# First two weight units in halves, feature rows one by one, and five products ahead on TensorE

## The chip, the cores and the metric

The kernel runs on one core of a Trainium2 chip. Its time is the device time of that core in microseconds (us), from the first to the last instruction. One execution is profiled; the others are only timed. In the names of the profile PE is TensorE's matmul, PEld its weight load, DVE is VectorE, ACT is ScalarE, POOL is GpSimd, SPq is SyncE's queue of DMA issues.

## What is computed

A trunk of two layers over 512 positions and 1024 features, in float32. Each layer adds half a feed-forward block, a mixer and another half of a feed-forward block to x, and an RMS norm ends the trunk. This case plays in the first feed-forward block:

```
def rmsnorm(x, w, eps=NORM_EPS):
    xf = x.astype(F32)
    y = xf * lax.rsqrt(jnp.mean(xf * xf, axis=-1, keepdims=True) + eps)
    return (y * w.astype(F32)).astype(x.dtype)

def swiglu(x, w_gate, w_up, w_down):
    return (jax.nn.silu(x @ w_gate) * (x @ w_up)) @ w_down
...
    for l in range(DEPTH):
        i = l // 2
        x = x + 0.5 * swiglu(rmsnorm(x, ffn_norm[l, 0]), ffn_w_gate[l, 0], ffn_w_up[l, 0], ffn_w_down[l, 0])
```

## The kernel before

x lies in `X` with features down the partitions: 8 rows of 128 features by 512 positions (256 KB each). The weights come in units. A unit of `w_gate` or `w_up` is 128 output features by 1024 inputs, 512 KB, and makes one bank of 128 by 512 results. Units alternate: 0 gate, 1 up, 2 gate, 3 up, and so on. SyncE loads units into the four slots of `RAW`, and a load waits until DVE has made the low part of the unit that held the slot (`lo_ready`).

Each product in full precision is done as three products on numbers split in two. ACT rounds the raw weights to the high part (`split_hi`, line 1340, counted by `hi_ready`), DVE subtracts it from the raw weights for the low part (`split_lo`, line 1989, counted by `lo_ready`). Both go to `WS`, which has two slots, so ACT may split unit 2 only when PE has done unit 0 (`unit_done`). x is split the same way into `H`, after a multiplication by the norm's weight: ACT line 1431 (`hhi_ready`), DVE line 2073 (`h_ready`). Of the pair of semaphores of such a name one counts even rows and one odd rows. For each of the 8 rows of a unit PE then does high by high, high by low and low by high (lines 614 to 616), 24 products of 512 columns in a unit.

The division by the root of the mean square is done on the results. So PE can start before it is known. ACT squares the rows of `X` (line 1350) into `US[:, 0]` and `US[:, 1]` in turn, DVE adds seven of them to `ACC` (line 2087), and `norm_sum` on PE (lines 655 and 656) sums `ACC` and the eighth over the features with two products in plain float32. ACT takes the root, DVE the reciprocal (line 2020), and then each bank is scaled, which sets it free. There are two gate and two up banks. POOL clears `ACC` at the very start (line 1860, `acc_clear`).

The order at the start is written by hand, engine by engine:
- SyncE: parameters (`PRM`), unit 0, x in four loads of two rows with unit 1 behind the first, unit 2, the constants (`CST`), unit 3.
- ACT and DVE: unit 0, rows 0 and 1, unit 1, rows 2 to 7, with squares between, then unit 2.
- PE (`first_units`): rows 0 and 1 of unit 0, rows 0 and 1 of unit 1, rows 2 to 7 of unit 0, rows 2 to 7 of unit 1; two rows of unit 2, `norm_sum`, the other six rows, unit 3. After this all phases go on by loops that count units.

## Time and profile before

| | us |
|---|---|
| median of 3 timed runs | 2102.22 |
| their range | 2101.36 to 2102.86 |
| the profiled execution (its span is its time) | 2102.0 |
| PE busy | 2062.4, 98% of the span |
| DVE busy | 1131.0, 54% |
| ACT busy | 780.5, 37% |

The profiled execution lies 0.2 us under the median. Starts are counted from the start of the span. In a timeline, a row gives start, length, engine, line, operation, what it writes and reads, and in brackets how long the engine had been idle and what ended that. Neighbours of one kind are merged into one row with a count. The lengths of pipelined products overlap, so what a product costs is read from the starts.

### The profile page before, as it was taken

To read this page: it belongs to the slowest core of one execution; us is meant where nothing else is said; L and a number is where in the kernel's file an instruction comes from. 1 tells how busy PE (TensorE), PEld (TensorE's weight loads), DVE (VectorE), ACT (ScalarE), POOL (GpSimd) and SP (SyncE) were. 2 spreads that over 40 slices of the span, in tenths; PEclk is the share of its full clock that TensorE was granted. 3 is DMA by queue.
4 is the path that set the end of the run, shared out by engine and by line. 5 is a ranking of instruction groups with operands and counts; after the bars stand their busy time and mean duration, and the time that the engine had idled before them with its cause. 6 is when DMAs were issued, how large, how long until landed. Compare 5 with 4: busy or idle time off the path is not lost.

```text
span 2102.0 us, 33182 instructions
## 1 busy us (share of the span) xinstructions
PE 2062.4 (98%) x13322; PEld 1699.5 (81%) x13322; DVE 1131.0 (54%) x1463; ACT 780.5 (37%) x1182; POOL 160.7 (8%) x118
## 2 busy tenths in 40 slices
PE   8999999999799999999999999999999999999998
PEld 6888888777768888888888888877888888888886
DVE  6444444678767444444444443469777675444322
ACT  5233223483434223322323232246665453233221
POOL 0000011002302000011000001101111120000010
PEclk9999999999999999999999999999999999999999
DMA  5222322320022222322222232221111122222321
GB/s 183 100 93 97 113 96 81 106 78 14 11 74 91 100 99 91 115 97 89 91 94 95 100 109 98 86 80 62 51 51 42 58 86 99 100 90 100 111 97 52
DMA packets 48265, 182.65 MB, mean 87 GB/s; under 512 B 6320, under 2 KB 6576, under 8 KB 48048
## 3 DMA queue, kind: packets, MB, share of 16 engines
q1 hardware_dynamic: 48176, 181.39, 25.1%
q8 instruction: 65, 1.06, 0.2%
q14 instruction: 24, 0.20, 0.0%
HBM read 179.27 MB, written 2.10 MB: 86 GB/s over the span
## 4 chain that ended last, share of the span: by engine, by line
PE 69%; DVE 2%; ACT 1%; issue 0%; POOL 0%; DVEq 0%; ACTq 0%; POOLq 0%
PE banks L614 21%; PE banks L615 21%; PE banks L616 21%; PE banks L1225 1%; PE banks L1194 0%; PE banks L1176 0%; PE banks L1264 0%; PE banks L1047 0%; PE banks L1266 0%; PE banks L1245 0%; PE banks L1242 0%; PE banks L1150 0%; PE banks L1130 0%; PE banks L1006 0%; DVE WS L1989 0%
## 5 line engine op out<-in xcount | busy, mean ns | idle before, releaser
L614 PE MATMUL banks<-H,WS 128*128 128x512 f32 x1840 | 727.6, 395 | 8.4 <-DVE H L2073 8.0
L615 PE MATMUL banks<-H,WS 128*128 128x512 f32 x1840 | 717.0, 390 | 0.0
L616 PE MATMUL banks<-H,WS 128*128 128x512 f32 x1840 | 716.9, 390 | 0.0
L1340 ACT ACTIVATE WS<-RAW 128x1024 fp32r<-128x1024 f32 (+1 forms) x306 | 345.0, 1128 | 909.4 <-PE banks L616 905.5
L1989 DVE TENSOR_TENSOR WS<-RAW,WS 128x1024 fp32r<-128x1024 f32 (+1 forms) x306 | 400.9, 1310 | 193.6 <-ACT WS L1340 193.2
L614 PEld LDWEIGHTS banks<-H,WS 128*128 128x128 f32 x1840 | 345.7, 188 | 85.1 <-DVE WS L1989 9.2
L616 PEld LDWEIGHTS banks<-H,WS 128*128 128x128 f32 x1840 | 345.7, 188 | 72.5
L615 PEld LDWEIGHTS banks<-H,WS 128*128 128x128 f32 x1840 | 345.9, 188 | 70.2 <-issue 1.2
L614 PE MATMUL banks<-A,WS 128*128 128x512 f32 x704 | 273.9, 389 | 0.0
L616 PE MATMUL banks<-A,WS 128*128 128x512 f32 x704 | 273.9, 389 | 0.0
L615 PE MATMUL banks<-A,WS 128*128 128x512 f32 x704 | 273.9, 389 | 0.0
L2029 DVE TENSOR_TENSOR US<-banks,RSTD 128x512 f32<-128x512 f32 x88 | 60.8, 691 | 252.2 <-PE banks L616 252.2
L1855 POOL TENSOR_TENSOR ACC<-ACC,US 128x512 f32<-128x512 f32 x47 | 87.5, 1862 | 1402.5 <-issue 763.0
L2029 DVE TENSOR_TENSOR GS<-banks,RSTD 128x512 f32<-128x512 f32 x88 | 60.8, 691 | 179.9 <-PE banks L616 179.8
L614 PEld LDWEIGHTS banks<-A,WS 128*128 128x128 f32 x704 | 132.1, 188 | 27.5
L616 PEld LDWEIGHTS banks<-A,WS 128*128 128x128 f32 x704 | 132.1, 188 | 27.5
L615 PEld LDWEIGHTS banks<-A,WS 128*128 128x128 f32 x704 | 132.1, 188 | 27.3
L2001 DVE SCALAR_TENSOR_TENSOR X<-banks,X 128x512 f32 (+1 forms) x48 | 33.0, 688 | 159.2 <-PE banks L616 159.2
L1380 ACT ACTIVATE A<-US 128x512 f32 (+1 forms) x88 | 55.8, 634 | 46.9 <-DVE US L2036 46.6
L2036 DVE TENSOR_TENSOR US<-GS,US 128x512 f32<-128x512 f32 x88 | 60.9, 692 | 9.1
L2041 DVE TENSOR_TENSOR A<-US,A 128x512 f32 (+1 forms) x88 | 60.2, 685 | 2.8 <-ACT A L1380 2.8
L1375 ACT ACTIVATE GS<-GS 128x512 f32<-128x512 f32 x88 | 54.1, 615 | 10.7 <-DVE GS L2029 10.7
(406 smaller groups left out, 1657.6 us busy)
## 6 DMA issues: line engine op xcount, KB each, us to landing
RAW<-in_w_gate SPq DMA_DIRECT2D x88, 512.0 KB, 3.2
RAW<-in_w_up SPq DMA_DIRECT2D x88, 512.0 KB, 3.2
RAW<-in_w_down SPq DMA_DIRECT2D x64, 704.0 KB, 4.0
RAW<-in_c_in SPq DMA_DIRECT2D x32, 512.0 KB, 3.2
RAW<-in_ab_in SPq DMA_DIRECT2D x22, 512.0 KB, 3.2
RAW<-in_ab_out SPq DMA_DIRECT2D x8, 512.0 KB, 5.0
RAW<-in_c_out SPq DMA_DIRECT2D x8, 512.0 KB, 3.2
X<-in_x SPq DMA_DIRECT2D x4, 512.0 KB, 7.5
```

The source lines that it names most:

```text
L614: pe.matmul(bank[:, :], high[:, cols], upper, start=first and j == 0, stop=False)
L615: pe.matmul(bank[:, :], high[:, cols], lower, start=False, stop=False)
L616: mm = pe.matmul(bank[:, :], low[:, cols], upper, start=False, stop=last and j == len(rows) - 1)
L1340: act.activation(WS[:, 0, c % SPLIT, 0:cols] if dst is None else dst, RAW[:, c % RING, 0:cols], ACT.Copy).then_inc(hi_ready, 1)
L1375: act.activation(GS[:, j, :], GS[:, j, :], ACT.Silu).then_inc(silu_ready[j], 1)
L1380: act.activation(A[:, 0, 2 * i + j, :], US[:, j, :], ACT.Copy).then_inc(ahi_ready[j], 1)
L1855: pool.tensor_tensor(ACC[:, :], ACC[:, :], US[:, j, :], ALU.add).then_inc(acc_ready[j], 1)
L1989: vec.tensor_tensor(WS[:, 1, c % SPLIT, 0:cols], RAW[:, c % RING, 0:cols], WS[:, 0, c % SPLIT, 0:cols].bitcast(F32), ALU.subtract).then_in ...
L2001: vec.scalar_tensor_tensor(X[:, 2 * i + j, :], bank[:, :], factor, X[:, 2 * i + j, :], ALU.mult, ALU.add).then_inc(x_ready[j], 1)
L2029: vec.tensor_tensor((GS, US)[k][:, j, :], (GATE, UP)[k][j][:, :], RSTD[:, :], ALU.mult).then_inc((gs_ready, us_ready)[k][j], 1)
L2036: vec.tensor_tensor(US[:, j, :], GS[:, j, :], US[:, j, :], ALU.mult).then_inc(prod_ready[j], 1)
L2041: vec.tensor_tensor(A[:, 1, 2 * i + j, :], US[:, j, :], A[:, 0, 2 * i + j, :].bitcast(F32), ALU.subtract).then_inc(act_ready[j], 1)
```

## The change

The first two units are loaded and split in two halves of 512 columns, that is of four input rows each. x is loaded row by row. Loads, splits and rows follow each other in one order on SyncE, ACT and DVE. PE takes rows 0 to 2 alternating between gate and up, then rows 3 to 7 of the gate unit and of the up unit, and waits for each row and half by itself. Ahead of all that PE does five products of 256 columns on the cleared `ACC`, into bank 7, which nobody reads; DVE waits for them before it adds to `ACC`. The squares all stand behind the last row now, with unit 2's split after the first two of them. `norm_sum` stands behind five rows of unit 2 and no longer behind two.

The diff:

```diff
--- before.py
+++ after.py
@@ -233,7 +233,12 @@
             return ctx.enter_context(nc.semaphore(name))
 
         landed = sem("constants_landed")
-        x_landed = [sem(f"x_landed{i}") for i in range(KB // 2)]
+        row_landed = [sem(f"row_landed{r}") for r in range(KB)]
+        params_landed = sem("params_landed")
+        half_landed = [sem(f"half_landed{c}") for c in range(2)]
+        half_hi, half_lo = [sem(f"half_hi{c}") for c in range(2)], [sem(f"half_lo{c}") for c in range(2)]
+        warmed = sem("warmed")
+        HALF_COLS = (slice(0, KB // 2 * P), slice(KB // 2 * P, KB * P))
         w_landed = [sem(f"weights_landed{s}") for s in range(RING)]
         hi_ready = sem("weights_hi_ready")
         lo_ready = sem("weights_lo_ready")
@@ -543,12 +548,25 @@
                     sp.wait_ge(lo_ready, u - RING + 1)
                 sp.dma_start(RAW[:, slot, 0:cols], src).then_inc(w_landed[slot], 16)
 
-            sp.dma_start(PRM[:, :], params).then_inc(x_landed[0], 16)
-            load(0, 0, *units[0])
-            for i in range(KB // 2):
-                sp.dma_start(X[:, 2 * i:2 * i + 2, :], x[:, 2 * i:2 * i + 2, :]).then_inc(x_landed[i], 16)
-                if i == 0:
-                    load(1, 1, *units[1])
+            def half_load(c, k):
+
+                sp.dma_start(RAW[:, c, HALF_COLS[k]], units[c][0][:, HALF_COLS[k]]).then_inc((half_landed, w_landed)[k][c], 16)
+
+            def row_load(r):
+
+                sp.dma_start(X[:, r, :], x[:, r, :]).then_inc(row_landed[r], 16)
+
+            half_load(0, 0)
+            sp.dma_start(PRM[:, :], params).then_inc(params_landed, 16)
+            row_load(0)
+            half_load(1, 0)
+            row_load(1)
+            row_load(2)
+            half_load(0, 1)
+            row_load(3)
+            half_load(1, 1)
+            for r in range(4, KB):
+                row_load(r)
             load(2, 2, *units[2])
             sp.dma_start(CST[:, :], const).then_inc(landed, 16)
             for phase in plan:
@@ -630,13 +648,34 @@
 
             def first_units(phase):
 
+                def row(k, r):
+
+                    pe.wait_ge(h_ready[r % 2], r // 2 + 1)
+                    if r < KB // 2:
+                        pe.wait_ge(half_lo[k], 1)
+                    else:
+                        pe.wait_ge(lo_ready, k + 1)
+                    bank, cols = (GATE[0], UP[0])[k], slice(r * P, (r + 1) * P)
+                    pe.matmul(bank[:, :], WS[:, 0, k, cols], H[:, 0, r, :], start=r == 0, stop=False)
+                    pe.matmul(bank[:, :], WS[:, 0, k, cols], H[:, 1, r, :], start=False, stop=False)
+                    mm = pe.matmul(bank[:, :], WS[:, 1, k, cols], H[:, 0, r, :], start=False, stop=r == KB - 1)
+                    if r == KB - 1:
+                        mm.then_inc(unit_done, 1)
+
+                pe.wait_ge(acc_clear, 1)
+                for _ in range(5):
+                    mm = pe.matmul(BANK[7][:, 0:SEQ // 2], ACC[:, 0:P], ACC[:, 0:SEQ // 2], start=True, stop=True)
+                mm.then_inc(warmed, 1)
                 c = base[phase]
-                for rows in ((0, 1), range(2, KB)):
-                    for k, bank in enumerate((GATE[0], UP[0])):
-                        unit(bank, c + k, 0, H_PARTS, rows, rows[0] == 0, rows[0] > 0, norm=0, at_col=rows[0], done=rows[0] > 0)
-                unit(GATE[1], c + 2, 0, H_PARTS, range(2), True, False, done=False)
+                for r in range(3):
+                    for k in range(2):
+                        row(k, r)
+                for k in range(2):
+                    for r in range(3, KB):
+                        row(k, r)
+                unit(GATE[1], c + 2, 0, H_PARTS, range(5), True, False, done=False)
                 norm_sum(0)
-                unit(GATE[1], c + 2, 0, H_PARTS, range(2, KB), False, True, at_col=2)
+                unit(GATE[1], c + 2, 0, H_PARTS, range(5, KB), False, True, at_col=5)
                 unit(UP[1], c + 3, 0, H_PARTS, range(KB), True, True)
 
             def norm_sum(n):
@@ -1423,23 +1462,34 @@
             step = Steps(act, act_step)
             act.wait_ge(acc_clear, 1)
             act.activation(SMALL[:, 0, :], ACC[:, 0:4], ACT.Square)
-            split_hi(0, 0)
-            for i in range(KB // 2):
-                act.wait_ge(x_landed[i], 32 if i == 0 else 16)
+            def half_split_hi(c, k):
+
+                act.wait_ge((half_landed, w_landed)[k][c], 16)
+                act.activation(WS[:, 0, c, HALF_COLS[k]], RAW[:, c, HALF_COLS[k]], ACT.Copy).then_inc(hi_ready if k else half_hi[c], 1)
+
+            def row_hi(r):
+
+                w = norm_cols[0] + r
+                act.wait_ge(row_landed[r], 16)
+                act.activation(H[:, 0, r, :], X[:, r, :], ACT.Copy, scale=PRM[:, w:w + 1]).then_inc(hhi_ready[r % 2], 1)
+
+            half_split_hi(0, 0)
+            act.wait_ge(params_landed, 16)
+            row_hi(0)
+            half_split_hi(1, 0)
+            row_hi(1)
+            row_hi(2)
+            half_split_hi(0, 1)
+            row_hi(3)
+            half_split_hi(1, 1)
+            for r in range(4, KB):
+                row_hi(r)
+            square(0, 0, 0)
+            square(0, 0, 1)
+            split_hi(2, 0)
+            for i in range(1, KB // 2):
                 for j in range(2):
-                    w = norm_cols[0] + 2 * i + j
-                    act.activation(H[:, 0, 2 * i + j, :], X[:, 2 * i + j, :], ACT.Copy,
-                                   scale=PRM[:, w:w + 1]).then_inc(hhi_ready[j], 1)
-                if i == 0:
-                    split_hi(1, 0)
-                if i == 1:
-                    for j in range(2):
-                        square(0, 0, j)
-            for i, j in ((1, 0), (1, 1), (2, 0)):
-                square(0, i, j)
-            split_hi(2, 0)
-            for i, j in ((2, 1), (3, 0), (3, 1)):
-                square(0, i, j)
+                    square(0, i, j)
             split_hi(3, 0)
             act.activation(SMALL[:, 1, :], PRM[:, 0:4], ACT.Sqrt, scale=0.0)
             for phase in plan:
@@ -2065,17 +2115,31 @@
                 vec.tensor_tensor(by_head(INV[z]["IU"]), two_banks(4 * z), minus_by_head(2 << l), ALU.mult).then_inc(iu_ready[z], 1)
 
             step = Steps(vec, vec_step)
-            split_lo(0, 0)
-            for i in range(KB // 2):
-                for j in range(2):
-                    w = norm_cols[0] + 2 * i + j
-                    vec.wait_ge(hhi_ready[j], i + 1)
-                    vec.scalar_tensor_tensor(H[:, 1, 2 * i + j, :], X[:, 2 * i + j, :], PRM[:, w:w + 1],
-                                             H[:, 0, 2 * i + j, :].bitcast(F32), ALU.mult, ALU.subtract).then_inc(h_ready[j], 1)
-                    vec.sem_inc(hw_ready[j], 1)
-                    vec.sem_inc(x_ready[j], 1)
-                if i == 0:
-                    split_lo(1, 0)
+            def half_split_lo(c, k):
+
+                vec.wait_ge(hi_ready if k else half_hi[c], c + 1 if k else 1)
+                vec.tensor_tensor(WS[:, 1, c, HALF_COLS[k]], RAW[:, c, HALF_COLS[k]],
+                                  WS[:, 0, c, HALF_COLS[k]].bitcast(F32), ALU.subtract).then_inc(lo_ready if k else half_lo[c], 1)
+
+            def row_lo(r):
+
+                w = norm_cols[0] + r
+                vec.wait_ge(hhi_ready[r % 2], r // 2 + 1)
+                vec.scalar_tensor_tensor(H[:, 1, r, :], X[:, r, :], PRM[:, w:w + 1],
+                                         H[:, 0, r, :].bitcast(F32), ALU.mult, ALU.subtract).then_inc(h_ready[r % 2], 1)
+                vec.sem_inc(hw_ready[r % 2], 1)
+                vec.sem_inc(x_ready[r % 2], 1)
+
+            half_split_lo(0, 0)
+            row_lo(0)
+            half_split_lo(1, 0)
+            row_lo(1)
+            row_lo(2)
+            half_split_lo(0, 1)
+            row_lo(3)
+            half_split_lo(1, 1)
+            for r in range(4, KB):
+                row_lo(r)
 
             def square_added(i, j):
 
@@ -2087,10 +2151,11 @@
                 vec.tensor_tensor(ACC[:, :], ACC[:, :], US[:, j, :], ALU.add).then_inc(acc_ready[j], 1)
 
             vec.wait_ge(acc_clear, 1)
-            for i, j in ((0, 0), (0, 1), (1, 0), (1, 1), (2, 0)):
-                square_added(i, j)
+            vec.wait_ge(warmed, 1)
+            square_added(0, 0)
+            square_added(0, 1)
             split_lo(2, 0)
-            for i, j in ((2, 1), (3, 0)):
+            for i, j in ((1, 0), (1, 1), (2, 0), (2, 1), (3, 0)):
                 square_added(i, j)
             vec.wait_ge(landed, 16)
             for phase in plan:
```

DVE's program, from its beginning. `WS<-RAW,WS` is a low part of weights (1024 columns are a unit, 512 a half), `H<-X,PRM,H` the low part of a feature row, `ACC<-ACC,US` a sum of squares. Before:

```order
L1989 TENSOR_TENSOR WS<-RAW,WS 128x1024
L2073 SCALAR_TENSOR_TENSOR H<-X,PRM,H 128x512 x2
L1989 TENSOR_TENSOR WS<-RAW,WS 128x1024
L2073 SCALAR_TENSOR_TENSOR H<-X,PRM,H 128x512 x6
L2087 TENSOR_TENSOR ACC<-ACC,US 128x512 x5
L1989 TENSOR_TENSOR WS<-RAW,WS 128x1024
L2087 TENSOR_TENSOR ACC<-ACC,US 128x512 x2
L1989 TENSOR_TENSOR WS<-RAW,WS 128x1024
```

And now:

```order
L2121 TENSOR_TENSOR WS<-RAW,WS 128x512
L2128 SCALAR_TENSOR_TENSOR H<-X,PRM,H 128x512
L2121 TENSOR_TENSOR WS<-RAW,WS 128x512
L2128 SCALAR_TENSOR_TENSOR H<-X,PRM,H 128x512 x2
L2121 TENSOR_TENSOR WS<-RAW,WS 128x512
L2128 SCALAR_TENSOR_TENSOR H<-X,PRM,H 128x512
L2121 TENSOR_TENSOR WS<-RAW,WS 128x512
L2128 SCALAR_TENSOR_TENSOR H<-X,PRM,H 128x512 x4
L2151 TENSOR_TENSOR ACC<-ACC,US 128x512 x2
L2039 TENSOR_TENSOR WS<-RAW,WS 128x1024
L2151 TENSOR_TENSOR ACC<-ACC,US 128x512 x5
```

Row 0 stands behind half a unit, not a whole one; unit 2's split stands behind two sums, not five.

SyncE's DMA issues at the start of the program, before (128x1024 is 512 KB):

```order
L546 DMA PRM<-in_params 128x243
L544 DMA RAW<-in_w_gate 128x1024
L549 DMA X<-in_x 128x1024
L544 DMA RAW<-in_w_up 128x1024
L549 DMA X<-in_x 128x1024 x3
L544 DMA RAW<-in_w_gate 128x1024
L553 DMA CST<-in_const 128x2112
```

And now:

```order
L553 DMA RAW<-in_w_gate 128x512
L560 DMA PRM<-in_params 128x243
L557 DMA X<-in_x 128x512
L553 DMA RAW<-in_w_up 128x512
L557 DMA X<-in_x 128x512 x2
L553 DMA RAW<-in_w_gate 128x512
L557 DMA X<-in_x 128x512
L553 DMA RAW<-in_w_up 128x512
L557 DMA X<-in_x 128x512 x4
L549 DMA RAW<-in_w_gate 128x1024
```

The bytes ahead of unit 2 are the same; they go out as 13 issues in place of 7.

## Rows read from the trace of the kernel before

**Rows 1.** The page's busy times, the first engine

```profile
PE 2062.4 (98%) x13322; PEld 1699.5 (81%) x13322; DVE 1131.0 (54%) x1463; ACT 780.5 (37%) x1182; POOL 160.7 (8%) x118
```

**Rows 2.** Timeline of PE, 0 to 25 us: start, length, what

```profile
7.95 0.77 PE L614 MATMUL banks<-H,WS 128*128 128x512 f32 x1 [7.95 <-DVE H L2073]
...
10.85 0.59 PE L614 MATMUL banks<-H,WS 128*128 128x512 f32 x1
11.28 0.40 PE L615 MATMUL banks<-H,WS 128*128 128x512 f32 x1
11.52 0.39 PE L616 MATMUL banks<-H,WS 128*128 128x512 f32 x1
...
20.40 0.39 PE L616 MATMUL banks<-H,WS 128*128 128x512 f32 x1
20.67 0.50 PE L614 MATMUL banks<-H,WS 128*128 128x512 f32 x1
...
22.16 1.05 PE L655 MATMUL banks<-ACC,CST 128*128 128x512 f32 x2
...
24.14 0.40 PE L615 MATMUL banks<-H,WS 128*128 128x512 f32 x1
```

**Rows 3.** Busy times by stretch: length, then PE, PEld, DVE, ACT, POOL, PEclk, DMA

```profile
7.95:10.65 2.70, 2.70 (x6) 1.80 (x6) 1.60 (x2) 1.93 (x3) 0.00 (x0) 1.00 0.99 352
...
515.00:526.00 11.00, 9.19 (x290) 8.92 (x284) 7.07 (x12) 1.73 (x3) 10.84 (x10) 0.84 0.01 4
```

**Rows 4.** Timeline of DVE, 5 to 30 us

```profile
7.06 1.41 DVE L2073 SCALAR_TENSOR_TENSOR H<-X,PRM,H 128x512 fp32r<-128x512 f32 x2
...
12.80 2.74 DVE L2073 SCALAR_TENSOR_TENSOR H<-X,PRM,H 128x512 fp32r<-128x512 f32 x4 [0.68 <-ACT H L1431]
15.46 3.87 DVE L2087 TENSOR_TENSOR ACC<-ACC,US 128x512 f32<-128x512 f32 x5
...
20.53 1.48 DVE L2087 TENSOR_TENSOR ACC<-ACC,US 128x512 f32<-128x512 f32 x2
...
24.86 3.35 DVE L2020 RECIPROCAL RSTD<-RSTD 128x512 f32<-128x512 f32 x1 [0.71 <-ACT RSTD L1369]
```

**Rows 5.** Timeline of ACT, 4 to 15 us

```profile
4.83 1.06 ACT L1340 ACTIVATE WS<-RAW 128x1024 fp32r<-128x1024 f32 x1 [2.59 <-DMA RAW<-in_w_gate]
6.10 1.33 ACT L1431 ACTIVATE H<-X,PRM 128x512 fp32r<-128x512 f32 x2 [0.21 <-DMA X<-in_x]
8.48 1.06 ACT L1340 ACTIVATE WS<-RAW 128x1024 fp32r<-128x1024 f32 x1 [1.05 <-DMA RAW<-in_w_up]
9.78 1.33 ACT L1431 ACTIVATE H<-X,PRM 128x512 fp32r<-128x512 f32 x2 [0.24 <-DMA X<-in_x]
...
12.06 2.55 ACT L1431 ACTIVATE H<-X,PRM 128x512 fp32r<-128x512 f32 x4
```

**Rows 6.** Timeline of SyncE's DMA issues: the first and the seventh

```profile
0.75 0.40 SPq L546 DMA_DIRECT2D PRM<-in_params  x1
...
3.75 0.45 SPq L549 DMA_DIRECT2D X<-in_x  x1
```

**Rows 7.** Those two in the DMA view: count, KB, us from issue to landing

```profile
PRM<-in_params SPq DMA_DIRECT2D x1, 121.5 KB, 2.2
...
X<-in_x SPq DMA_DIRECT2D x1, 512.0 KB, 8.7
```

**Rows 8.** The page's groups: 512-column operations of the split's kind

```profile
L1380 ACT ACTIVATE A<-US 128x512 f32 (+1 forms) x88 | 55.8, 634 | 46.9 <-DVE US L2036 46.6
...
L2041 DVE TENSOR_TENSOR A<-US,A 128x512 f32 (+1 forms) x88 | 60.2, 685 | 2.8 <-ACT A L1380 2.8
```

**Rows 9.** Timeline of POOL: the clearing of the accumulator

```profile
0.74 0.52 POOL L1860 MEMSET ACC<- 128x512 f32 x1 [0.29 <-POOLq L2687]
```

**Rows 10.** DMA view, 2.0 to 12.4 us, then 381.8 to 384.3 us

```profile
DMA packets 1076, 3.65 MB, mean 351 GB/s; under 512 B 115, under 2 KB 210, under 8 KB 1073
...
DMA packets 309, 0.63 MB, mean 253 GB/s; under 512 B 32, under 2 KB 32, under 8 KB 309
```

## The prediction

> **What bounds the kernel now.** I read the page's busy times first: TensorE (PE) is busy for 98% of the span [rows 1]. A microsecond saved elsewhere is worth nothing unless PE stood waiting for it, and one saved ahead of PE's first product reaches the end in full if no later wait swallows it. So the second view is PE's timeline at the start. The first product of the kernel starts at 7.95 us, and until then PE has done nothing. After that the reader should look at the step from one product to the next. At 10.85 it is 0.43 us (to 11.28), which is 512 columns at 1.2 GHz; from 11.52 to 20.40 there are 39 steps, so 0.228 us each, the 2.4 GHz level [rows 2]. The opening 6 products take the 2.70 us from 7.95 to 10.65. The granted-clock column reads 1.00 there too, so here the steps show the clock and the column does not [rows 3]. Third, the engines that feed PE. VectorE (DVE) has the low part of the last feature row at 12.80 + 2.74 = 15.54 us [rows 4]. ScalarE (ACT) takes each piece the moment it lands, at 4.83, 6.10, 8.48 and 9.78 us, each time after a wait on a DMA [rows 5]. So the opening is bound by arriving data.
>
> From 7.95 to unit 2's first product at 20.67 lie 48 products, 12.72 us; at 0.228 us they need 10.94. Thus 1.78 us go to the slow clock and to waits, and 0.12 more behind 20.67, where six steps of 0.228 take 1.49 us to 22.16 [rows 2].
>
> **Arrival.** Bytes queued decide arrivals. Cumulated in queue order in KB: parameters 122, unit 0 634, first x pair 1146, unit 1 1658, second pair 2170, third 2682, fourth 3194. They land at 0.75 + 2.2 = 2.95 us (parameters), 4.83, 6.10, 8.48, 9.78 (ACT's starts), and the last at 3.75 + 8.7 = 12.45 [rows 5 to 7]. The change queues the same bytes in halves; seven issues went out in the 3.0 us to 3.75, so an issue costs 0.5 us, 256 KB per 0.5 us, faster than the data moves (351 GB/s) [rows 6, 10]. I therefore read the new landings off the same curve, by straight lines between its points: gate half 3.44, row 0 at 4.83, up half 5.46, row 1 at 6.10, row 2 at 7.29, second gate half 8.48, row 3 at 9.13, second up half 9.78, rows 4 to 7 at 10.45, 11.1, 11.8 and 12.45. For the 256 KB of the gate half this is an estimate from the rows at 2.95 and 4.83.
>
> **Cost of the pieces.** A 512-column split is not in the opening, but the same operation on a 512-column tile is: 0.634 us on ACT and 0.685 on DVE [rows 8]. A feature row is 0.71 us on ACT, at a pace of 2.55/4 = 0.64; on DVE 0.746, pace 2.74/4 = 0.685 [rows 4, 5]; one engine's instructions overlap by some 0.07 us. ACT has the gate half at 4.07 and row 0 at 4.83 + 0.71 = 5.54; DVE the gate half's low part at 4.8 and row 0 at 6.32. Before, row 0's low part was ready at 7.06 + 0.75 = 7.81 and PE started 0.14 later. **So the first product comes at 6.46 instead of 7.95: 1.49 us.** What goes is the wait for the whole unit's two splits, of which the second blocked DVE until 7.1 us.
>
> **The race behind it.** Carried on the same way, DVE ends the up half at 6.93, row 1 at 7.61, row 2 at 8.78, row 3 at 10.62, row 4 at 11.94, rows 5 to 7 at 12.6, 13.3 and 13.98. A row of one unit is 3 products, 0.683 us. From 6.46 PE does rows 0 to 2 of both units in 4.10 us, to 10.56; waits 0.16 for row 3 and 0.64 for row 4 (ready 11.94 + 0.1); then finds rows 5, 6 and 7 as it arrives. Row 7 starts at 14.1, and 6 row steps are left: unit 2 could start at 14.1 + 6 x 0.683 = 18.2. **Sum of this stretch: 1.49 (start) + 1.78 (old losses) - 0.80 (new waits) = 2.47 us.** New waits are late data, not weights.
>
> **The five products** read the cleared accumulator, ready at 0.74 + 0.53 = 1.27 us [rows 9]. Their cost is bounded by the kernel's own products in this number form: two of 512 columns fill 22.16 to 24.14 less one 0.228 step, 0.88 us each at 2.4 GHz [rows 2]. At half the columns 0.44, at half the clock 0.88; five take 4.4 us, to about 5.8, under the 6.46 at which data is there. I take that value. The upper end is 1.76 us each, if 256 columns took as long as 512, which ends at 10.1. No lower end matters, because they hide under the data wait. What they buy is the clock: before, the fast level came at about 11.3 us, after seven products had kept PE busy nearly without a break since 7.95; the five keep it busy from 1.4 to 5.8 us, for longer, and end before the data is there, so I take the fast level from 6.46 on. DVE's new wait for them stands behind row 7 (13.98 us), long after: nothing.
>
> **Unit 2, the squares and the norm.** ACT may split unit 2 when unit 0 is done, 14.1 + 0.68 + 0.15 = 14.95, to 16.0; DVE to 17.3; PE wants it at 18.2. Covered by 0.9 us, and the old 0.12 goes. Then five sums remain on DVE, 3.87 us by the row of five [rows 4], to 21.1. PE, with five rows of unit 2 ahead of the sum over features, comes there at 18.2 + 5 x 0.683 = 21.6: covered by 0.5 us (before, 22.01 against 22.16). The extra three rows ahead of it are only moved, but they delay the sum: it starts 0.55 us earlier, not 2.5. The reciprocal behind it ended at 24.86 + 3.35 = 28.2 [rows 4], now at about 27.65, and its first bank is drained by 28.4. PE needs that bank after 3 + 8 more row steps, 21.6 + 1.75 + 7.5 = 30.9. Slack 2.5 us. The loads of units 4 and later start by DVE's splits and arrive long before use. Nothing after this point is touched.
>
> **Sum:** 2.47 + 0.12 = 2.59 us off the profiled execution's 2102.0: 2099.4. That execution is 0.2 us under the median of the timed runs and 0.66 above the fastest, so I take its sum as it is.
>
> **A rule against the trace.** The last 3194 KB land without a fixed cost between pieces: 512 KB takes 1.27 us from 4.83 to 6.10 [rows 5]. The Trainium skill, DMA: Bandwidth & Descriptors, Rules for kernel authors, asks for at least 1 MiB per DMA for bandwidth, and its section on the anatomy of one DMA fits 2.0 us plus the bytes at 436 GB/s; its rule speaks against halves. If the fixed parts did not overlap, 13 transfers would cost an estimated 30 us or more by that page and the kernel would end near 2120; this trace disagrees for queued transfers, so the rule only stands beside rival C.
>
> **The rivals.**
> - A, the forecast: 2099.4.
> - B, **the clock is not up when the data comes.** Between the five products (5.8) and the first real one lies an idle 0.7 us, and the early rows have waits. In 515 to 526 us of this trace the granted clock is 0.84 amid waits and small products [rows 3], so it can fall. If it stays at 1.2 GHz until 11.3 as before, 4.8 us run at half speed, 2.4 us lost, of which 0.8 falls into the data waits: +1.6, 2101.0. Against it: before, the clock rose through six products with a short wait among them.
> - C, **the halves move slower; this one ends above before.** Rows of 2 KB instead of 4 KB on the memory side. Until 12.4 us 3.65 MB moved at 351 GB/s; in a stretch with 2 KB loads in it, 253 GB/s [rows 10]. At that rate the same bytes take 14.4 us from 2.0, row 7 lands at 16.4 and not 12.45, and all behind it moves by 4.0: 2103.4. It decides from about 280 GB/s on (row 7 at 15.0 is break-even); beyond 0.2% slower it would have to be near 210. Against it: that stretch has just started its queue and carries still smaller pieces.
> - D, **more than forecast.** If rows come so smoothly that PE never waits, 0.8 us more; if the run resembles the fastest of before (0.66 lower), 2098.0. For it: the slow stretch of before may last longer in executions other than the profiled one. The Trainium skill, TensorE: Matmul & The Clock Gate, says that the number of slow matmuls at a kernel's start varies from run to run (Part 1, on the clock gate); it gives 6, 11 and 14 for one kernel. By that page alone an estimate is up to 8 x 0.2 = 1.6 us of more gain. One trace can't show it.
> - E, **the five products hold PE.** At 1.76 us each the first real product waits until 10.1, then runs fast: unit 2 at 21.0, 2102.3.
> - F, **the gain is given back later:** unit 3's split or the bank of unit 4 late after all. 2102.0.
>
> **How the numbers follow.** A 0.70, B 0.08, C 0.04, D 0.12, E 0.03, F 0.03. Predicted 2099.4. The range 2097.8 to 2101.6 holds A, B and D, and leaves C, E and F out, 0.1 plus what may lie outside by unknown cost. A measurement of this kernel tells 0.2% from no change, 4.2 us: below 2098.0 or above 2106.4. Faster by that: most of D, 0.10. Slower by that: half of C, 0.02. Within: 0.88.
>
> **What would show it.** In the profile after: first real product near 6.5; step 0.228 from there or from shortly after; small waits before rows 3 and 4, none by weights; row 7's low part near 14.0; unit 2's first product near 18.2; no wait at the feature sum. A row 7 landing past 13 us speaks for C, steps of 0.43 after 6.5 for B, a first product after 7 with idle DVE for E. The prediction is wrong if the 16 DMA engines don't serve the halves in the order queued, since every time above hangs on that curve.

## The result: 6.5 us slower

| | before | after |
|---|---|---|
| median of 7 timed runs, us | 2102.03 | 2108.52 |
| their range | 2101.33 to 2102.86 | 2107.25 to 2109.36 |
| span of the profiled execution | 2102.0 | 2106.6 |

The ratio is 1.003 with a 95% interval of 1.0021 to 1.0039. 2.6 us of gain were forecast. In every run here the time lies about 1.8 us above the span (2108.42 and 2106.6 for the profiled execution of after). The profiled execution of before is therefore not a typical one: by its span of 2102.0 its time must be near 2103.8, above all seven timed runs, and it holds a stretch at the lower clock at 520 us (granted clock 0.56 from 519.4 to 523.3). A second trace of the same kernel (b_again, span 2099.6, time 2101.41) lacks that stretch, and I compare with it where it says so; its time lies 0.4 to 1.1 us under the medians of before, so it is one of the faster ones. Two executions of b_tail32 (2307 and 4862 us) and one of before beside them (2566 us) were disturbed and are left out below.

**Where the time went.** I laid the starts of ScalarE's some 300 weight splits of the two traces side by side; how late a kernel is by this measure I call its lag. Against b_again, after is about 2.8 us late from 40 us on and stays so until 490 us; in the first mixer, 495 to 600 us, it loses 4.2 more; after that nothing changes up to the end: 7.0 = 2106.6 - 2099.6. So there are two places, the opening and the mixer, and the second has not one edited line in it.

**The first place.** The timeline of PE in after: start, length, line, what it writes and reads, and in brackets how long it was idle and what ended that. The five products are the first row (ten records).

```profile
1.32 3.98 PE L667 MATMUL banks<-ACC 128*128 128x256 f32 x10 [1.32 <-POOL ACC L1910]
6.86 0.50 PE L659 MATMUL banks<-H,WS 128*128 128x512 f32 x1 [1.57 <-DVE H L2128]
7.20 0.40 PE L660 MATMUL banks<-H,WS 128*128 128x512 f32 x1
...
8.86 0.47 PE L659 MATMUL banks<-H,WS 128*128 128x512 f32 x1 [1.02 <-DVE WS L2121]
...
13.54 0.50 PE L659 MATMUL banks<-H,WS 128*128 128x512 f32 x1 [0.30 <-DVE H L2128]
...
19.87 0.39 PE L632 MATMUL banks<-H,WS 128*128 128x512 f32 x1
...
23.27 1.02 PE L694 MATMUL banks<-ACC,CST 128*128 128x512 f32 x2
...
34.46 0.50 PE L632 MATMUL banks<-H,WS 128*128 128x512 f32 x1 [1.79 <-DVE WS L2039]
...
35.29 0.63 PE L632 MATMUL banks<-H,WS 128*128 128x512 f32 x1
...
38.67 0.39 PE L634 MATMUL banks<-H,WS 128*128 128x512 f32 x1
```

PE begins at 6.86 in place of 7.95 [rows 2], runs at 2.4 GHz at once (7.20 to the next at 7.44), and reaches unit 2 at 19.87, 0.8 ahead of before. The sum over features (L694) comes at 23.27, 1.1 later than the 22.16 of before: three more rows stand ahead of it, 2.05 us of work, which use up the lead of 0.8 and more. (Without them it could have come 0.4 sooner at most, since DVE's last sum, which it needs, ends at 22.80; see a_norm2.) At unit 4 PE waits 1.79 us for DVE's low part. Then, from 35.29 to 38.67, eight steps take 3.38 us, 0.42 each: the 1.2 GHz level. Eight at 0.228 are 1.82, so this costs 1.56 more. The same unit began at 33.52 in before, without a wait; 34.46 - 33.52 + 1.56 = 2.5 us. PE's timeline and DVE's in before, unit 4's first product and its split:

```profile
33.52 0.50 PE L614 MATMUL banks<-H,WS 128*128 128x512 f32 x1
```

```profile
32.24 1.22 DVE L1989 TENSOR_TENSOR WS<-RAW,WS 128x1024 fp32r<-128x1024 f32 x1
```

DVE's timeline in after says why unit 4 is late.

```profile
12.73 2.77 DVE L2128 SCALAR_TENSOR_TENSOR H<-X,PRM,H 128x512 fp32r<-128x512 f32 x4
15.42 1.48 DVE L2151 TENSOR_TENSOR ACC<-ACC,US 128x512 f32<-128x512 f32 x2
17.79 1.22 DVE L2039 TENSOR_TENSOR WS<-RAW,WS 128x1024 fp32r<-128x1024 f32 x1 [0.89 <-ACT WS L1379]
18.93 3.87 DVE L2151 TENSOR_TENSOR ACC<-ACC,US 128x512 f32<-128x512 f32 x5
...
25.81 3.35 DVE L2070 RECIPROCAL RSTD<-RSTD 128x512 f32<-128x512 f32 x1 [0.86 <-ACT RSTD L1408]
...
32.59 0.68 DVE L2079 TENSOR_TENSOR GS<-banks,RSTD 128x512 f32<-128x512 f32 x1
33.19 1.22 DVE L2039 TENSOR_TENSOR WS<-RAW,WS 128x1024 fp32r<-128x1024 f32 x1
```

The last feature row's low part ends at 15.50, before at 15.54 [rows 4]: all that begins earlier ahead of it ends at the same time. Behind it DVE even falls back. Only two of its sums now stand ahead of unit 2's low part, and that waits for ACT's split (16.70, itself released by PE's end of unit 0), so DVE idles 0.89 us before 17.79; in before five sums stood there, until 19.33 [rows 4], and the low part followed at 19.39. Its last sum ends at 22.80 against 22.01, and root and reciprocal follow (25.81 against 24.86 [rows 4]), then the scalings of units 0 and 1, and behind them stands unit 4's split, 33.19 to 34.41.

**The second place** is seen in waits that the profile lays to "issue", which means that nothing it shows was waited for. PE's timeline from 495 to 605 us in after has three:

```profile
535.38 0.33 PE L774 MATMUL banks<-IU,XT 64*64 64x64 f32 x2 [1.02 <-issue]
567.13 0.45 PE L774 MATMUL banks<-IU,XT 64*64 64x64 f32 x12 [1.15 <-issue]
580.60 0.62 PE L1014 MATMUL banks<-VT,KBT 64*64 64x64 f32 x14 [0.96 <-issue]
```

b_again has one, at the same product as the third:

```profile
573.61 0.62 PE L975 MATMUL banks<-VT,KBT 64*64 64x64 f32 x14 [0.95 <-issue]
```

Here PE runs hundreds of products of 64 columns. Behind the first stall of after the clock is low: 32 such products take 1.13 us at 537.02 and 0.69 at 542.13 (timeline of after).

```profile
537.02 1.13 PE L774 MATMUL banks<-IU,XT 64*64 64x64 f32 x32
...
542.13 0.69 PE L774 MATMUL banks<-IU,XT 64*64 64x64 f32 x32
```

The stalls are 3.1 us against 0.95, so 2.2 of the 4.2; the rest, 2.0, is this stretch (granted clock 0.66 from 536 to 541 us) and what waits for it, which I did not divide further. The third stall is no part of the loss: it stands at the same product, the 8852nd from the end of PE's program, and lasts 0.95 to 0.96 us in every one of the fourteen traces of this case.

**The loads.** DMA by stretch, 4 to 7 us, in before and then in after (length; busy us of PE, PEld, DVE, ACT, POOL; clock; share of the DMA engines; GB/s):

```profile
4.00:7.00 3.00, 0.00 (x0) 0.00 (x0) 1.08 (x1) 1.96 (x3) 0.00 (x0) 1.00 0.99 344
```

```profile
4.00:7.00 3.00, 1.43 (x6) 0.88 (x5) 1.44 (x2) 0.89 (x2) 0.00 (x0) 1.00 0.79 216
```

The halves and rows start well and then fall behind. The single rows of x have a share in this: in the same stretch the other kernels that load them so have 243 to 260 GB/s (a_split4, a_trim_nowarm, a_nowarm), a_pairs, which has half weights but x in pairs, has 325, and b_again 391. ACT's timeline in after shows when it could take what had landed: gate half 3.54, row 0 at 5.30, up half only at 7.35.

```profile
3.54 0.63 ACT L1468 ACTIVATE WS<-RAW 128x512 fp32r<-128x512 f32 x1 [1.30 <-DMA RAW<-in_w_gate]
5.30 0.72 ACT L1474 ACTIVATE H<-X,PRM 128x512 fp32r<-128x512 f32 x1 [1.13 <-DMA X<-in_x]
7.35 0.63 ACT L1468 ACTIVATE WS<-RAW 128x512 fp32r<-128x512 f32 x1 [1.33 <-DMA RAW<-in_w_up]
```

### The profile page after: what moved, and what is told of

Same layout as the page of the kernel before. It is cut to its first block, busy times and chain, and to the rows that moved or that the text cites. A ratio compares the mean times of both kernels' runs of the same rounds, so it can differ in the third digit from the quotient of the medians.

```text
span 2106.6 us, 33225 instructions
## 1 busy us (share of the span) xinstructions
PE 2067.7 (98%) x13332; PEld 1703.3 (81%) x13332; DVE 1132.4 (54%) x1465; ACT 781.4 (37%) x1184; POOL 160.7 (8%) x118
## 4 chain that ended last, share of the span: by engine, by line
PE 69%; DVE 2%; ACT 1%; issue 0%; POOL 0%; DVEq 0%; ACTq 0%; POOLq 0%
PE banks L632 21%; PE banks L633 21%; PE banks L634 21%; PE banks L1264 1%; PE banks L1233 0%; PE banks L1215 0%; PE banks L1303 0%; PE banks L1086 0%; PE banks L1305 0%; PE banks L1284 0%; PE banks L1281 0%; PE banks L1189 0%; PE banks L1169 0%; PE banks L1045 0%; DVE HF L2740 0%
```

## The experiments

The two theories: S, **the split of unit 4** stands at the end of a chain that the change made end later, while PE comes there earlier (theory 1 in the expectations below); P, **the place in the program** (theory 3): the change puts 32 instructions into PE's program ahead of the mixer (20 for the five products, 12 for rows that wait for two semaphores; of 64 bytes each, by the length of the compiled program, 1,073,216 bytes before and 2048 more after), and at which products PE has to wait for its instructions depends on that. Their rivals were the five products themselves, the smaller loads (theory 2), and chance from run to run. The runs came in three groups with runs of before on the same chip beside them, whose medians were 2102.52 (26 runs), 2101.79 (15) and 2102.51 (35).

### a_split4: after, unit 4's split ahead of the scalings

```diff
+                        elif first:
+                            split_hi(4, 0)
...
+                        if first and not base[phase]:
+                            split_lo(4, 0)
                         scaled(phase, i, j, 0)
```

At its old place, behind the scalings, unit 4's split is left out on both engines; that part of the edit is not shown.

> The changed kernel with one thing moved: on ScalarE and VectorE the split of weight unit 4 stands right behind the root and the reciprocal, ahead of the first bank's scaling, and no longer behind it. Theory 1 (the feature sum comes 1.1 us later than before, since five rows of unit 2 stand ahead of it, and with it unit 4's split; PE then waits 1.79 us at 32.5 us and its clock falls to the lower level for 8 products, 1.6 us): the wait and the slow stretch are gone, the time is 3.4 us under the changed kernel, about 2105.1. Theory 2 (the halved loads are slow and that is all): no difference, 2108.5. Theory 3 (the five products or the longer program cost time in later phases): no difference here either.

Measured: 2107.76 (2104.63 to 2110.44, 10 runs), ratio 1.0023 (1.0014 to 1.0033); profiled span 2104.3. The wait at unit 4 is gone from the trace, as DVE's timeline shows: the split is the first thing behind the reciprocal.

```profile
26.57 3.36 DVE L2072 RECIPROCAL RSTD<-RSTD 128x512 f32<-128x512 f32 x1 [0.84 <-ACT RSTD L1408]
29.96 1.22 DVE L2041 TENSOR_TENSOR WS<-RAW,WS 128x1024 fp32r<-128x1024 f32 x1
```

At 390 us this execution is level with b_again (-0.1 us), though it fell to the lower clock once in its first waits (steps of 0.43 from 9.35 to 11.91). In the mixer it then loses 4.8. So the trace bears S out for the first place; S says nothing of the second. The timed runs alone don't show it: the median moved by 0.8 where 3.4 were expected, and the interval overlaps that of after. Three of the ten runs lie at 2104.6 to 2104.9 with a mean granted clock of 0.998, the others at 2106.1 and more with 0.995 to 0.997, so the low clock comes and goes between runs. The timed proof of S is the last experiment.

### a_norm2: after, the sum over features behind two rows again

```diff
-                unit(GATE[1], c + 2, 0, H_PARTS, range(5), True, False, done=False)
+                unit(GATE[1], c + 2, 0, H_PARTS, range(2), True, False, done=False)
                 norm_sum(0)
-                unit(GATE[1], c + 2, 0, H_PARTS, range(5, KB), False, True, at_col=5)
+                unit(GATE[1], c + 2, 0, H_PARTS, range(2, KB), False, True, at_col=2)
```

> The changed kernel with the feature sum behind two rows of unit 2, as before, instead of five. Theory 1: PE gets there at 21.2 us and waits for the sums of squares, which end at 22.8, so the sum starts at 22.9 instead of 23.27; unit 4's split comes 0.4 us earlier and the total waits of PE are about the same: 2108.1, between 2106.5 and 2108.5. If instead the five rows alone were the cause, the feature sum would start near 21.3 and the time come out at 2104 or less.

Measured: 2109.39 (2106.80 to 2112.79, 7 runs), ratio 1.0035 (1.0024 to 1.0047). PE's timeline:

```profile
23.13 1.10 PE L694 MATMUL banks<-ACC,CST 128*128 128x512 f32 x2 [1.54 <-DVE ACC L2151]
```

The wait at unit 4 is gone and stands at the sum instead, 1.54 us. The sum starts at 23.13 where it started at 23.27: DVE sets it, not PE. Taking the three rows away brings the sum only 0.14 us; what then holds it is DVE's last sum, which ends at 23.03 in this trace behind a gap of 1.96 ahead of unit 2's low part. PE's lead can be taken back at either place, but it is taken back. The time is above the 2106.5 to 2108.5 that I expected: the opening of this execution loses only 1.3 us against b_again, with no low clock behind the wait, but the mixer 6.3, with a fourth stall.

### a_nowarm: after without the five products

```diff
-                pe.wait_ge(acc_clear, 1)
-                for _ in range(5):
-                    mm = pe.matmul(BANK[7][:, 0:SEQ // 2], ACC[:, 0:P], ACC[:, 0:SEQ // 2], start=True, stop=True)
-                mm.then_inc(warmed, 1)
```

> The changed kernel without the five products ahead and without VectorE's wait for them. Theory 1: the first products run at the lower clock for some 3.4 us from 6.9 us on, the waits for rows swallow a part; PE reaches the feature sum up to 1 us later (up to 24.3 us), and everything behind follows: 2108.5 to 2109.5. Theory 3 (these products cost time later by the longer program): up to 2 us faster, 2106.5.

Measured: 2107.76 (2106.19 to 2108.75, 8 runs), ratio 1.0025 (1.0014 to 1.0036). The first 6.5 us of products go at 0.43 each, unit 2 comes at 21.21, and unit 4's wait of 1.79 us is there to the digit, with the lower clock behind it. In the mixer, where its displacement is 12 instructions in place of 32, it loses 1.8 and not 4.2. In the traces the five products win about 1.3 us at unit 2, and 2.4 more are lost in the mixer with the 20 instructions that they are; the two medians (0.8 apart) have intervals that overlap.

### b_warm: before with the five products and DVE's wait for them, nothing else

```diff
+                pe.wait_ge(acc_clear, 1)
+                for _ in range(5):
+                    mm = pe.matmul(BANK[7][:, 0:SEQ // 2], ACC[:, 0:P], ACC[:, 0:SEQ // 2], start=True, stop=True)
+                mm.then_inc(warmed, 1)
...
             vec.wait_ge(acc_clear, 1)
+            vec.wait_ge(warmed, 1)
```

> The kernel before with nothing but the five products ahead (and VectorE's wait for them). PE starts at full clock at 7.95 us and could be 1.2 us ahead at the end of the first two units. Theory 1 (the chain of splits, sums, root, reciprocal and unit 4's split on VectorE bounds the opening, PE's lead is taken back at unit 2's split, ready at 20.6 us): nothing gained, 2102.0, within 0.5; a fall of the clock in the new wait could make it 1 to 2 us slower. If PE alone bounded the opening: 2100.8. Theory 3 (later phases pay for the longer program): 2103.5 to 2104.

Measured: 2104.65 (2103.54 to 2107.70, 10 runs), ratio 1.0011 (1.0001 to 1.0021). At 390 us it is 0.3 ahead of b_again, so the clock gain at the start was real, and most of it was taken back: a wait of 0.53 for the up unit's weights, then unit 2 at 20.06 right behind the end of its low part (20.01), 0.6 ahead, and unit 4 at 32.91, right behind the end of its own (32.86), 0.6 ahead. In the mixer it loses 3.5. **This is an edit of the first microseconds whose cost lies in the mixer, with a stall of 1.34 at 562 us.**

### b_pad32 and b_pad128: before with increments of an unused semaphore at PE's head

```diff
+                for _ in range(32):
+                    pe.sem_inc(warmed, 1)
                 c = base[phase]
```

> The kernel before with 32 semaphore increments that nobody waits for at the head of PE's program, where PE is idle until 8 us; its PE program is then exactly as long as the changed kernel's (32 instructions of 64 bytes more). Theory 3, sharpened (PE's instructions are fetched in pieces of 16 KB, and in the mixer stretch at 500 to 600 us, with many short products, PE stands still where a fetch comes late; a longer head moves these places): the opening is as before, the stretch 500 to 600 us has the changed kernel's stalls of issue (3.1 us against 1.6 in the profile before), 1.5 to 3 us slower, 2104 to 2105.5. Theory 1 alone (only the opening matters): 2102.5, as before.

Measured: 2107.62 (2106.51 to 2108.53, 9 runs), ratio 1.0027 (1.0017 to 1.0037). The loads, splits, products and their order are those of before, and PE was idle where the increments stand. The loss, 5.8 us, is nearly that of the whole change and more than the 1.5 to 3 I expected. PE's timeline from 495 to 605 us:

```profile
533.48 0.32 PE L738 MATMUL banks<-IU,XT 64*64 64x64 f32 x2 [1.02 <-issue]
546.70 0.33 PE L867 MATMUL banks<-FACTORS,AL 64*64 64x64 f32 x5 [1.13 <-issue]
565.88 0.45 PE L738 MATMUL banks<-IU,XT 64*64 64x64 f32 x12 [1.15 <-issue]
579.35 0.62 PE L978 MATMUL banks<-VT,KBT 64*64 64x64 f32 x14 [0.96 <-issue]
```

The first, third and fourth are the three of after: the same products (2 left of one group, 12 of another), the same lengths. The second has none beside it in after, but one in a_norm2. 0.9 us are lost in the opening, 4.8 in the mixer.

b_pad128 has `range(128)` there.

> The same with 128 increments, half a piece of 16 KB. Theory 3: other stalls again, a time that differs from the kernel before and from the one with 32, between 2102 and 2106. Theory 1 alone: 2102.5.

Measured: 2117.50 (2117.25 to 2119.23, 4 runs), ratio 1.0075 (1.0059 to 1.0092). This one is half spoilt as a test: the 128 increments last until 20.50 us, 0.16 each, and so hold PE's first product back by 12 us. Behind that the mixer loses 3.1. Two stalls stand at other products again (1.56 at 545.47, 1.10 at 575.89); the third (589.88) is the one that all traces have.

### b_again: before once more

> The kernel before once more, for a second profile: the first has a stretch at the lower clock in the mixer (519.9 to 523.3 us) and lies 1.3 us above the median of the timed runs of before. Expected span 2100.7, without that stretch; the stalls of issue in 500 to 600 us at the same lines as in the first profile if they belong to the program.

Measured: 2101.41, span 2099.6, no stretch at the lower clock at 520 us. Of the first trace's three stalls (0.21 at 531.19, 0.43 at 560.78, 0.95 at 576.20) only the last is there; so a place decides where a stall can fall, not that it does.

### a_pairs: after with x in four loads of two rows

```diff
-                sp.dma_start(X[:, r, :], x[:, r, :]).then_inc(row_landed[r], 16)
+                sp.dma_start(X[:, r:r + 2, :], x[:, r:r + 2, :]).then_inc(row_landed[r], 16)
```

> The changed kernel with x loaded in four pairs of rows, as before, and only the weights in halves; the rest of the order is the same. Theory 2 (the many 256 KB transfers carry the data more slowly: 170 to 254 GB/s in 4 to 7 us against 266 to 414 before): the up half and rows 1 to 3 land up to 1 us earlier and PE reaches unit 2 at about 19.0 instead of 19.9 us; but the time follows the chain of the sums (row 7's low part) only, so 0 to 0.9 us faster, 2107.6 to 2108.5. If halves of weights alone make the slow stretch: no difference in landings.

Measured: 2109.40 (2106.43 to 2111.42, 7 runs), ratio 1.0034 (1.0022 to 1.0045), profiled span 2104.6. In its trace the feature sum comes at 22.21, 1.1 earlier than in after, and unit 4 still waits 1.79, to 33.41. By 390 us it is 0.2 behind b_again, with no low clock behind that wait, and loses 4.8 in the mixer. So eight loads of x cost about a microsecond in the opening of the profiled execution; the median, 0.9 above that of after and above what I expected, shows none of it.

### b_tail32: before with the 32 increments behind PE's last product

```diff
             mm.then_inc(rows_ready, 1)
+            for _ in range(32):
+                pe.sem_inc(warmed, 1)
```

> The kernel before, with 32 increments of an unused semaphore behind the last product of TensorE's program instead of ahead of its first: the program has the length of the changed kernel's, but every instruction up to the last product stands where it stood before. Theory (what counts is the place of the mixer's instructions in the program, because it decides at which products the stalls that wait for instructions fall): 0.0 us, median 2101.5 to 2102.8, in the mixer (495 to 605 us) the stalls of the kernel before, 1.0 to 1.6 us in all. Rival (the length or the loading of a longer program costs, wherever the instructions stand): +5 us, as with 32 increments at the head, about 2107.

Measured: 2102.18 (2101.58 to 2103.04, 10 runs), ratio 0.9998 (0.9989 to 1.0008). **The same 32 instructions cost 5.8 us at the head and nothing at the end.** In the mixer:

```profile
529.41 0.46 PE L736 MATMUL banks<-IU,XT 64*64 64x64 f32 x16 [0.22 <-issue]
558.79 0.62 PE L736 MATMUL banks<-IU,XT 64*64 64x64 f32 x26 [0.17 <-issue]
574.21 0.62 PE L976 MATMUL banks<-VT,KBT 64*64 64x64 f32 x14 [0.96 <-issue]
```

### b_pad12: before with 12 increments at the head

```diff
+                for _ in range(12):
+                    pe.sem_inc(warmed, 1)
                 c = base[phase]
```

> The kernel before with 12 increments at the head of TensorE's program, the same displacement as that of the changed kernel without its five products. Theory (place in the program): the mixer is 1.8 us later than in the other execution of before, as there, and the opening is at most 0.4 later since TensorE has nothing to do until 7 us: 2103.5 to 2105. Rival (a stall comes by chance from execution to execution, not by place): 2102 plus 0 to 0.4, the spans spread as those of before.

Measured: 2105.07 (2102.48 to 2106.39, 11 runs), ratio 1.0011 (1.0002 to 1.0020). At 390 us its lag is 0.3; in the mixer 3.8, twice what I expected; it also falls to the lower clock there (granted clock 0.98 from 495 to 605 us, where a_nowarm has 1.00). PE's timeline:

```profile
529.70 0.51 PE L738 MATMUL banks<-IU,XT 64*64 64x64 f32 x19 [0.27 <-issue]
562.86 0.33 PE L738 MATMUL banks<-IU,XT 64*64 64x64 f32 x2 [1.29 <-issue]
577.73 0.62 PE L978 MATMUL banks<-VT,KBT 64*64 64x64 f32 x14 [0.96 <-issue]
```

The size of the term can't be had from the displacement alone.

### a_trim_nowarm: after without the five products and without 20 waits that repeat one already passed

```diff
-                    pe.wait_ge(h_ready[r % 2], r // 2 + 1)
-                    if r < KB // 2:
+                    if k == 0:
+                        pe.wait_ge(h_ready[r % 2], r // 2 + 1)
+                    if r == 0:
                         pe.wait_ge(half_lo[k], 1)
-                    else:
+                    elif r == KB // 2:
                         pe.wait_ge(lo_ready, k + 1)
```

> The changed kernel without the five products, and without the waits of TensorE in the opening that repeat one already passed (a row's wait only for the gate unit, a half's wait only at its first row): TensorE's program is then 2 instructions shorter than before, in place of 12 longer. Theory (place): the mixer costs what it costs in the kernel before, 0 to 0.5 us of lag in place of 1.8, and the opening keeps the 3.9 us that it loses without the five products (a clock fall behind the wait at unit 4 among them): 2105.5 to 2106.5, 1.5 to 2 less than the kernel without the five products (2107.8). Rival (the mixer's share has nothing to do with the place): no difference from 2107.8.

Measured: 2105.20 (2102.58 to 2106.08, 11 runs), ratio 1.0012 (1.0003 to 1.0021): 2.6 us less than a_nowarm, by leaving out waits for what is already there. How much of it is the opening, the medians don't say. PE's program loses 14 instructions by it and is 2 shorter than before's. The profiled execution is the fastest of the eleven: its mixer loses 0.5 and its opening only 1.1, because the lower clock did not follow unit 4's wait this time. PE's timeline there, then a_nowarm's at the same place:

```profile
34.29 0.50 PE L632 MATMUL banks<-H,WS 128*128 128x512 f32 x1 [1.79 <-DVE WS L2036]
34.63 0.40 PE L633 MATMUL banks<-H,WS 128*128 128x512 f32 x1
...
35.80 0.39 PE L632 MATMUL banks<-H,WS 128*128 128x512 f32 x1
36.03 0.40 PE L633 MATMUL banks<-H,WS 128*128 128x512 f32 x1
```

```profile
35.81 0.50 PE L632 MATMUL banks<-H,WS 128*128 128x512 f32 x1 [1.79 <-DVE WS L2035]
...
37.13 0.63 PE L634 MATMUL banks<-H,WS 128*128 128x512 f32 x1
37.56 0.63 PE L632 MATMUL banks<-H,WS 128*128 128x512 f32 x1
```

With the bare wait this kernel is 1.1 us behind b_again in the opening, and the clock behind the wait costs 1.6 more where it falls. That it fell in most of the other ten is a reading of their times only.

### a_trim_nowarm_split4: both causes taken away

This is a_trim_nowarm with the edit of a_split4.

> The kernel of a_trim_nowarm, with unit 4's split right behind the root on ScalarE and behind the reciprocal on VectorE, ahead of the scalings. Theory (two causes, the wait at unit 4 and the place in the program, both taken away): no wait at unit 4, no clock fall behind it, the mixer as before: 0 to 0.5 us off or on to the kernel before, 2101.8 to 2103, unless the clock falls in one of the waits of the first 15 us (then +1.5, 2104). Rival (row loads and halves cost more than these two explain): 2105 and above.

Measured: 2101.77 (2100.75 to 2102.34, 11 runs), ratio 0.9996 (0.9987 to 1.0005). There is no wait at unit 4, and in the mixer two stalls are left (PE's timeline):

```profile
529.08 0.46 PE L771 MATMUL banks<-IU,XT 64*64 64x64 f32 x15 [0.21 <-issue]
573.52 0.62 PE L1011 MATMUL banks<-VT,KBT 64*64 64x64 f32 x14 [0.95 <-issue]
```

**Halves, row loads and the alternating order are all in it, and the 6.5 us are gone.** Unit 4's split alone is the 3.4 us between this kernel and a_trim_nowarm; their ranges of eleven runs each do not overlap. It does not beat before measurably. It is 0.4 ahead of b_again at 390 us, although its data comes earlier: DVE's chain sets the end of the opening.

### The mixer, by how far PE's program is displaced

| kernel | instructions ahead of the mixer | "issue" stalls, 495 to 605 us | granted clock there | lag added in the mixer against b_again |
|---|---|---|---|---|
| a_trim_nowarm, with split4 | -2 | 1.4, 1.2 | 1.00, 1.00 | 0.5, 0.3 |
| b_again, b_tail32, before | 0 | 0.95, 1.35, 1.6 | 1.00, 1.00, 0.98 | 0, 0.6, 2.3 |
| a_nowarm, b_pad12 | +12 | 2.0, 2.5 | 1.00, 0.98 | 1.8, 3.8 |
| b_warm | +20 | 2.3 | 0.98 | 3.5 |
| after, a_split4, a_pairs, b_pad32, a_norm2 | +32 | 3.1, 3.7, 3.1, 4.3, 5.0 | 0.98, 0.98, 0.97, 0.98, 0.98 | 4.2, 4.8, 4.8, 4.8, 6.3 |
| b_pad128 | +128 | 3.6 | 1.00 | 3.1 |

One stall of 0.95 is in every row and explains no difference. What the lag has beyond the stalls goes with the clock: 0.1 to 0.8 us where it reads 1.00, 1.5 to 2.6 where it reads 0.97 or 0.98. The clock is not the place's doing alone, since before falls at 519.5 us, ahead of its first stall.

Kernels of one displacement stall at the same products, whatever else differs in them, though not every one has every stall. Where the other stalls stand follows the displacement by a rule that can be counted in PE's records of matmuls. A product of this kind is two records and four instructions (b_warm's five products are ten records and 20 instructions). In before two stalls stand 10468 and 9390 records from the end. With 2 instructions fewer they stand one record later (10467, 9389), with 12 more the first stands six earlier (10474): half the displacement each time. All others of these two stand at the place so shifted and then exactly 126 records later: 9270 at +12, 9274 at +20, 10358 and 9280 at +32, 10406 and 9328 at +128. By two instructions a record, 126 records are 252 instructions, nearly the 256 that 16 KB hold; whether four instructions without such a record make up the difference was not checked. So these stalls keep to places a fixed distance apart, counted from the start of PE's program, and a longer head moves them to other products. What PE waits for is an inference all the same: the page of after lists instruction transfers,

```profile
q8 instruction: 65, 1.06, 0.2%
```

65 pieces of 16 KB, about the length of PE's program, and while the 64-column products run one comes about every 4 us. The Trainium skill, Runtime: NRT & Kernel Launch, section Terms, says that an engine's instruction memory is refilled in blocks of 16 KiB; the sizes in this trace agree. Why a stall comes at some blocks and not at others stays open, as do displacements below -2.

## Why the prediction was wrong, point by point

- **The start of PE, -1.49.** Measured -1.09 (6.86). ACT took the gate half at 3.54 for 3.44, row 0 at 5.30 for 4.83.
- **Arrival of what follows.** The up half was put at 5.46 and came at 7.35, because the transfer curve of before was taken over unchanged; 216 GB/s in place of 344 from 4 to 7 us. Rival C's reason was true for this stretch. From 8 to 12 us the rate was near that of before (362 against 367, and 419 in b_again, so two executions of one kernel differ by more), and rival C's 4 us didn't come: the last low part ended at 15.50, as before. The Trainium skill's rule on the size of a DMA (DMA: Bandwidth & Descriptors, Rules for kernel authors), set aside in the prediction, has the trace on its side from 4 to 7 us; the estimate of 30 us or more made from that page's fit is nowhere near, and the page gives the fit for DMAs that GpSimd issues, while these are SyncE's. New waits: 1.32 us (1.02 + 0.30) in place of 0.80, and one of them by weights, which the prediction had excluded.
- **The five products.** 0.80 us each (3.98 for five) against 0.88, and the fast level from the first product: right in this execution. Luck has a part in it: a_split4 and a_norm2 have the same opening up to there and fell to the lower level among the first rows (9.35 to 11.91 and 9.02 to 11.15 us). Unit 2 at 19.87 and not 18.2.
- **The feature sum at 21.6, covered by 0.5.** It came at 23.27. DVE's last sum ended at 22.80, so 0.47 of cover: right in the cover, wrong by 1.7 us in the place, since the low parts ended at 15.50 and not at 13.98 and unit 2's low part at 19.01 and not at 17.3. That the cover came out right is luck: PE and DVE were late by nearly the same.
- **"Slack 2.5 us."** This is the failed step of the opening. It asked when the first bank is free for unit 4 and not when unit 4's weights are split. The row was there to be read: in before PE starts unit 4 at 33.52 and DVE's split ends at 33.46, no slack at all. In after PE is there at 32.67, 0.85 earlier, and the split ends at 34.41, 0.95 later, because the sum is 1.1 later. Two things hold the sum at nearly the same time: PE's rows until 23.27, and DVE's last sum, behind its gap of 0.89, until 22.80. Seen from the sum: the change takes three rows of unit 2, 9 x 0.228 = 2.05 us of PE's work, out from behind the sum and puts them ahead of it; the way from the sum to unit 4's first product is as long as ever (11.19 us after, 11.36 before). The wait that came is 1.79 us, and it is 1.79 in a_nowarm, a_trim_nowarm and a_pairs too, whenever their data comes.
- **The clock.** Rival B had it fall among the first rows; here it fell behind unit 4's wait and cost 1.56. That B's 1.6 is so near is luck, since it was worked out for another stretch. The fall among the first rows came in two of the five traces that have the five products (a_split4, a_norm2), so B's 0.08 was too low.
- **"Nothing after this point is touched."** The failed step of the rest, and the larger one: 4.2 of 7.0 us. No rival had it. Every term of the sum counted what an instruction does, and none where it stands. b_pad32 and b_tail32 show the term by itself: 5.8 us and nothing, with the same 32 instructions.
- **The base.** The sum was made against a span of 2102.0 taken as a time. That execution's time is near 2103.8, and its mixer is 2.3 us slower than b_again's, 0.6 of it in two stalls and the rest at its stretch of low clock. The two errors nearly cancel, so the base did little harm.
- The chance of "slower by over 0.2%", 0.02, rested on one mechanism that is not the one that came. Even without the mixer the change would have been 2 to 3 us slower by my estimate from the opening's 2.8 and from a_trim_nowarm (2.7 above its before), inside the 0.2%.

## What to carry to other kernels

When work is moved across a synchronisation, count what it used to cover behind it, and ask of every consumer behind it for all its inputs, bank and weights alike. An engine's early lead is worth only as much as the chain that it meets next; here VectorE's chain from the last feature row to unit 4's split ended when it ended. In a kernel like this one, whose TensorE program is long and has dense stretches of small products, an edit ahead of them can cost microseconds by its count of instructions alone: compare the "issue" waits of both traces, and run a control that adds as many idle instructions at the same place, and one that adds them at the end.

## What the runs showed of the hardware

- 32 idle instructions at the head of a program of 16,769 cost 5.8 us of 2102 (interval of the ratio 1.0017 to 1.0037), and nothing at its end (0.9989 to 1.0008). The stalls that move with them stand 126 records of matmuls apart. 20 waits that are always fulfilled already (14 instructions) cost 2.6 us in a_nowarm.
- Two waits on one product take a second instruction on PE: taking the second wait from 14 of 16 products in the opening made the compiled program 14 instructions shorter. An increment on PE takes 0.16 us (128 of them ended at 20.50).
- After the same wait of 1.79 us at unit 4 PE's steps went to the 1.2 GHz level in after (35.29 to 38.67) and in a_nowarm, and stayed at 2.4 GHz in a_trim_nowarm and a_pairs. Behind the stalls of the mixer too the level fell in some traces and not in others. The column of the granted clock shows these stretches (0.50 from 35.3 to 38.6 us in after), but not the slow first products of before, where it reads 1.00 [rows 3], nor those of a_nowarm (1.00 from 7 to 13 us); there only the steps do.
- A float32 product of 256 columns took 0.80 us in the first 5 us of after, as two records each, and 0.78 to 0.93 in the five traces that have it.
- SyncE's issue of the last four rows of x took 3.13 us, 0.78 each, where the first ones took 0.43 (2.66 to 3.16 us for the four in a_split4, a_nowarm and a_trim_nowarm). Why was not tested.

```profile
1.67 0.42 SPq L557 DMA_DIRECT2D X<-in_x  x1
...
4.98 3.13 SPq L557 DMA_DIRECT2D X<-in_x  x4
```
